# Four buffers for the late modulation weights, roots finished on VectorE, one weight split taken ahead

## What is computed

```python
c_act = silu(c)
for layer in range(2):
    mod = c_act @ w_ada[layer] + b_ada[layer]            # 1024 x 3072: shift, scale, gate
    h = rms(x, norm_g[layer]) * (1 + scale) + shift
    ...                                                  # layer 0: gated delta; layer 1: w_ada_kv (1024 x 2048) too
    x = x + gate * y

def gdn_mixer(h, w_in, conv_w, ...):
    proj = h @ w_in                                      # 1024 x 4112
    qkv = silu(causal_conv(proj[..., :3072], conv_w))
    z = proj[..., 3072:4096]
    q = l2norm(q per head of 128) * 128 ** -0.5
    k = l2norm(k per head of 128)
    # chunks of 64 tokens: a triangular inverse for each chunk and head, then a scan over the chunks
    return (rms(o) * silu(z)) @ w_out
```

## Time and profile before

| | us |
|---|---|
| median of 3 runs | 1294.51 (1293.77 to 1295.87) |
| the profiled execution, device time | 1292.0 |
| span of its trace | 1290.1 |
| TensorE busy in it | 1199.9 (93%) |
| opening, to the start of block 1 on TensorE | 70.2 |
| blocks 1 to 5, the z stage and its waits, to the start of the inverses (first L2173) | 70.2 to 254.6 |
| inverses with the late modulation, to the start of the scan (first L2263) | 254.6 to 378.8 |
| scan and all later layers | 378.8 to 1290.1 |

### The profile page before, as it was taken

One profiled execution on the slowest core, in us unless ns is written; L12 is line 12 of the kernel. 1 busy time (PEld: TensorE's weight loads), 2 busy tenths in 40 slices (PEclk: granted clock), 3 DMA queues, 4 the chain that ended last, 5 costly groups with the idle time before them and its releaser, 6 DMA issues.

```text
span 1290.1 us, 20510 instructions
## 1 busy us (share of the span) xinstructions
PE 1199.9 (93%) x8602; PEld 906.3 (70%) x8602; DVE 452.0 (35%) x852; ACT 541.0 (42%) x916; POOL 378.1 (29%) x150
## 2 busy tenths in 40 slices
PE   5899998989889889999998998989999999999989
PEld 3688875667658767777775656757887677777767
DVE  4575533343314214260214553140202333231563
ACT  4132238733326233452547663233134533654430
POOL 0134431322145442334431000423144213343331
PEclk7999998999999899999998999999999999999999
DMA  9533331156570221223321100233132412224201
GB/s 324 173 92 98 98 98 33 34 184 207 173 228 2 98 66 66 98 66 103 109 99 49 23 12 1 68 102 98 33 114 66 139 41 66 69 95 139 93 1 66
DMA packets 105613, 120.05 MB, mean 93 GB/s; under 512 B 5128, under 2 KB 91560, under 8 KB 105528
## 3 DMA queue, kind: packets, MB, share of 16 engines
q1 hardware_dynamic: 101280, 114.37, 28.0%
q10 hardware_dynamic: 4248, 4.45, 1.2%
HBM read 111.47 MB, written 2.10 MB: 88 GB/s over the span
## 4 chain that ended last, share of the span: by engine, by line
PE 82%; ACT 6%; DMA 4%; DVE 4%; issue 3%; SPq 1%; ACTq 0%; DVEq 0%
PE ps L1851 47%; PE ps L2545 4%; PE ps L2387 2%; PE ps L2396 2%; PE ps L1940 1%; DMA raw<-in_w_ada_kv_dram 1%; PE ps L2420 1%; PE ps L1974 1%; DMA raw<-in_w_ada_dram 1%; PE ps L2514 1%; PE ps L2027 1%; PE ps L2196 1%; PE ps L2501 1%; PE ps L2461 1%; PE ps L2607 1%
## 5 line engine op out<-in xcount | busy, mean ns | idle before, releaser
L556 POOL TENSOR_TENSOR wlo<-raw,whi 128x2048 fp32r<-128x2048 f32 x55 | 253.6, 4611 | 606.7 <-ACT whi L714 594.3
L714 ACT ACTIVATE whi<-raw 128x2048 fp32r<-128x2048 f32 x54 | 103.2, 1910 | 247.4 <-PE ps L1851 207.2
L562 POOL TENSOR_TENSOR wlo<-raw,whi 128x2048 fp32r<-128x2048 f32 x10 | 46.3, 4632 | 117.3 <-ACT whi L813 117.3
L1177 ACT ACTIVATE p<-sc,nmx 128x256 f32<-128x256 f32 x64 | 31.9, 501 | 57.9 <-DVE nmx L1682 57.9
L1851 PE MATMUL ps<-hC_hi,whi 128*128 128x512 f32 x208 | 52.9, 396 | 0.0
L1851 PE MATMUL ps<-hC_lo,whi 128*128 128x512 f32 x208 | 51.4, 389 | 0.0
L1851 PE MATMUL ps<-hC_hi,wlo 128*128 128x512 f32 x208 | 51.4, 389 | 0.0
L813 ACT ACTIVATE whi<-raw 128x2048 fp32r<-128x2048 f32 x12 | 23.0, 1916 | 63.8 <-PE ps L1851 63.8
L1851 PEld LDWEIGHTS ps<-hC_hi,whi 128*128 128x128 f32 x208 | 38.3, 188 | 14.9 <-issue 7.2
L1851 PEld LDWEIGHTS ps<-hC_lo,whi 128*128 128x128 f32 x208 | 39.0, 188 | 8.3
L1851 PEld LDWEIGHTS ps<-hC_hi,wlo 128*128 128x128 f32 x208 | 39.0, 188 | 8.1
(11 more groups left out here) (456 smaller groups left out, 2741.1 us busy)
## 6 DMA issues: line engine op xcount, KB each, us to landing
raw<-in_w_in_dram SPq DMA_DIRECT2D x24, 1024.0 KB, 5.1
raw<-in_w_in_a_dram SPq DMA_DIRECT2D x16, 1024.0 KB, 5.5
raw<-in_w_ada_dram SPq DMA_DIRECT2D x16, 1024.0 KB, 5.2
raw<-in_w_ada_kv_dram SPq DMA_DIRECT2D x8, 1024.0 KB, 5.7
raw<-in_w_kv_dram SPq DMA_DIRECT2D x8, 1024.0 KB, 5.3
raw<-in_w_in_b_dram SPq DMA_DIRECT2D x8, 1024.0 KB, 5.4
ada_a<-in_w_ada_dram SPq DMA_DIRECT2D x4, 1024.0 KB, 12.3
ada_b<-in_w_ada_dram SPq DMA_DIRECT2D x4, 1024.0 KB, 12.6
```

The costliest lines, as they stand in the source:

```text
L556: pool.tensor_tensor(wlo[:, s, :], raw[:, s, :], whi[:, s, :].bitcast(F32), ALU.subtract).then_inc(lo_ready, 1)
L562: pool.tensor_tensor(wlo[:, s, :], raw[:, s, :], whi[:, s, :].bitcast(F32), ALU.subtract).then_inc(lo_ready, 1)
L714: A(whi[:, s, :], raw[:, s, :], ACT.Copy).then_inc(hi_ready, 1)
L1177: A(p2[:, n % 2, 256 * e:256 * e + 256], sc2[:, n % 2, 256 * e:256 * e + 256], ACT.Exp, scale=-1.0, bias=nmx[:, grp, t, 2 * hp + e:2 * hp ...
```

## The change

Four edits, all in the first layer.

1. `late_w`, two further buffers of 1 MB in place of `hA_lo` (free once the z stage is multiplied). The late units of odd `ada` number go there, the others stay in `raw`. A load waits for the last use of its own buffer, which is now four units back; the first two of `late_w` wait for the end of block 7 (`dense_full`). They count on semaphores of their own (`ada_loaded[s]`). The loads of block 8 wait for units 20 and 21 in place of 22 and 23.
2. `root_halves` has one logarithm and two exponentials; `lengths` waits for both exponentials of the pair, copies the 64 rows of the root to the other half on VectorE, waits for its own copy (`roots_moved`), and multiplies.
3. The high part of block 1's first unit is taken between `hA_hi` tiles 5 and 6, behind a wait for its load. The GpSimd part has its place and its wait (`hi_ready`) unchanged.
4. GpSimd waits for `xin_done` 2 (both transposes of the first head pair) ahead of `decayed_queries(0)`.

```diff
+            with ExitStack() as s2:
+                sb("pad_lw", [128, KD * T], F32, s2)
+                late_w = sb("late_w", [128, 2, 2048], F32, s2)
...
+        def spare(what, n):
+
+            return what == "ada" and (n - EARLY) % 2 == 1
...
             def raw_free(r, s):
 
-                what, n = order[r - 1]
+                of = [load for load in order[:r] if spare(*load) == spare(*order[r])]
+                if not of:
+                    sp.wait_ge(dense_full, 4 * D_OUTA)
+                    return
+                what, n = of[-1]
                 sp.wait_ge(ada_done if what == "ada" else lo_ready, 2 * n + s + 1)
...
-                        dst = raw_ch(s)
-                    sp.dma_start(dst, src).then_inc(raw_loaded[s], 16)
+                        dst = late_src(n, s) if what == "ada" else raw_ch(s)
+                    sp.dma_start(dst, src).then_inc((ada_loaded if spare(what, n) else raw_loaded)[s], 16)
...
             restores(0, (0, 1))
+            pool.wait_ge(xin_done, 2)
             decayed_queries(0)
...
                 A(second, gdn_bank(g), ACT.Ln, bias=epsc).then_inc(ss_read, 2)
                 act.wait_ge(ss_read, g + 2)
-                A(first[64:128, :], second[0:64, :], ACT.Exp, scale=-0.5)
                 A(first[0:64, :], second[0:64, :], ACT.Exp, scale=-0.5).then_inc(r_ready, 1)
-                act.wait_ge(r_ready, g + 1)
-                A(second[0:64, :], second[64:128, :], ACT.Exp, scale=-0.5).then_inc(rh_read, 1)
-                act.wait_ge(rh_read, (g - G_GDN) // 2 + 1)
                 A(second[64:128, :], second[64:128, :], ACT.Exp, scale=-0.5).then_inc(r_ready, 1)
...
             for k in range(KD):
+                if k == KD - 2:
+                    act.wait_ge(raw_loaded[0], 32)
+                    A(whi[:, 0, :], raw[:, 0, :], ACT.Copy).then_inc(hi_ready, 1)
                 act.wait_ge(xr_done, k + 1)
                 act.wait_ge(mods_pair, 2 * (k // 2) + 2)
                 A(hA_hi[:, k, :], xr[:, k, :], ACT.Identity, scale=amul[:, 0, k:k + 1],
...
             def lengths(t0, t1):
                 for t in range(t0, t1):
-                    dve.wait_ge(r_ready, G_GDN + t + 1)
+                    dve.wait_ge(r_ready, G_GDN + t - t % 2 + 2)
+                    here, there = side(t % 2), side(1 - t % 2)
+                    copy(rbuf[there, (G_GDN + t) % 2, :], rbuf[here, (G_GDN + t) % 2, :]).then_inc(roots_moved, 1)
+                    dve.wait_ge(roots_moved, t + 1)
                     STT(qkvT[:, t, :], qkvT[:, t, :], 128.0 ** -0.5 if t < HG else 1.0, rbuf[:, (G_GDN + t) % 2, :],
                         ALU.mult, ALU.mult).then_inc(qkn_done, 1)
```

More of the change, by code:

```diff
@@ L293, in raw_ch, with raw_count, spare_count, late_src @@
             return raw[:, s, :].rearrange("p (k n) -> p k n", k=KD)
+        def spare(what, n):
+            return what == "ada" and (n - EARLY) % 2 == 1
+        def raw_count(what, n):
+            return 16 * sum(not spare(*load) for load in order[:load_of[what, n] + 1])
+        def spare_count(n):
+            return 16 * (1 + (n - EARLY + 1) // 2)
+        def late_src(n, s):
+            return late_w[:, s, :].rearrange("p (k n) -> p k n", k=KD) if spare("ada", n) else raw_ch(s)
         def modrow(o):
```

17 lines of the change are left out of this document (10 added, 7 removed).

## The result

The kernel before took 1295.19 us in the median beside the changed kernel (1293.77 to 1296.70, 4 runs), the changed kernel 1278.91 us (1275.07 to 1286.65, 4 runs). The ratio is 0.9882, with a 95% interval of 0.9834 to 0.9930. Its profiled execution took 1279.78 us, with a span of 1277.8.

A forecast was written before the change was run, and what follows sets the result against it. TensorE carries 82% of the chain, so only its standstills pay. Gains of 5.6 + 0.6 + 1.0 + 10.8 = 18.0 us take the median from 1294.5 to 1276.5 us, range 1272.0 to 1283.0.

The forecast's parts named there:

- The four waits that I chose: TensorE's waits: 4.92 us in the opening, 5.21 before block 7, 4.19 before the inverses, 10.8 for late modulation weights.
- Opening, -5.6: Block 1's first unit split ahead: tile 7's low part no longer held, no clock drop; block 1 starts 5.6 us earlier.
- Roots, -0.6: z stage: two exponentials fewer per pair against two VectorE copies of 0.42 us; z_silu(0) 0.6 us earlier.
- rival 3: z stage: GpSimd's split goes ahead of VectorE's fourth scaling and holds it, delaying the gates; 1279.5 us, chance 0.12.
- Queries, -1.0: Before the inverses: GpSimd's queries no longer hold a select, -1.0 us; bound +0.2 if select L1472 is held beside them.
- Four buffers, -10.8: Late units, 270 to 378 us: loads may start four units before, so all ten DMA waits go, 10.8 us.
- each wait is saved whole: Late units: at each of the ten waits the other engine was done before the weights, so nothing replaces the wait.
- rival 1: Late stretch: waits without releaser, from many short TensorE instructions, take back 5.8 us; 1282.3 us, chance 0.14.
- Rival 2: Late stretch: the 2.9 us wait without releaser goes too, 2.9 and 1.3 us more gained; 1272.3 us, chance 0.08.
- Rivals 4 and 5: 4: single queue makes the buffers useless, 1287.3 us, chance 0.05; 5: seven 2.9 us waits, slower, 1296.8 us, chance 0.01.
- Behind the scan, as long as before: Layers behind the scan: the scan starts 18.0 us earlier, and all behind it takes as long as before, 911 us.
- The signs of being wrong: Waits without releaser growing between 255 and 370 us, or a first unit's copy waiting for its load.

The follow-up runs named there:

- no_opening_split: The changed kernel with block 1's first weight copy put back behind tile 8, the other three edits kept; 1285.93 us, 0.9924 of the kernel before.
- after_third: The changed kernel run once more, unchanged, in the third group of experiments; 1277.28 us, 0.9846 of the kernel before.
- after_again: The changed kernel run once more, unchanged, in the first group of experiments; 1280.19 us, 0.9885 of the kernel before.
- four_exponentials: The changed kernel with the roots as before (four exponentials on ScalarE, no copies on VectorE); 1277.51 us, 0.9839 of the kernel before.
- z_wait: The changed kernel with GpSimd's second z block split waiting for six norm inputs; run twice, 1277.81 and 1273.39 us, 0.9854 and 0.9824 of the kernel before.
- no_pool_wait: The changed kernel without GpSimd's wait for the transposes' inputs ahead of the decayed queries; 1282.11 us, 0.9902 of the kernel before.
- two_buffers: The changed kernel with all late units in the two raw buffers again (no late_w); 1288.94 us, 0.9936 of the kernel before.

## Why the prediction was right, and where it was off

- **What bounds the kernel**: right. The four waits that I chose were the four that changed, and the scan starts 15.0 us earlier in the first profile.
- **Opening, -5.6**: right; 4.25 us of wait and 1.35 of clock by no_opening_split, less up to 0.7 for a hold that I put at 0.1; 5.5 at block 1 in the kernel after. Two details were off. The load was issued 0.6 us later than in the kernel before and landed as much later, so the copy waited for it (0.84 us, and 0.43 in after_third) and began at 47.45 and not at 47.2. And L1292, now L1313, was held 0.76 us and not 0.1, since the split ended at 54.05 and not at 53.7, and since VectorE came to it 0.6 us earlier than before (53.15, not 53.77). TensorE came 0.7 us later to tile 6 for it. In after_third the hold was 0.36 (0.52 less 0.16) and cost 0.3; in after_again, where the split ended at 53.56, it was nothing. In the first profile the TensorE clock hid this: the kernel before was at half clock from 18 to 35 us and this one wasn't.
- **Roots, -0.6**: mechanism right, size off; 0.2 to 0.3. The step that failed is the gate product, which I had ending 0.2 us earlier. The split did start 0.16 earlier measured from block 1, but took 4.80 us in place of 4.60, so the product ended where it had. It began at 198.40, while VectorE's last scaling of the pair (198.05 to 198.74) ran, which the two copies had put there; in four_exponentials, where VectorE was idle at its start, it took 4.62. So the likely reason is the same hold the other way round, which I had left out; no run tests it apart. I had the fourth logarithm 0.7 later, and it was 1.07. The chain through the held product was right; I priced the edit in it, but didn't say that removing the hold would be worth ten times as much as the edit (2.8 against 0.25). The hold of 2.94 us stood in the earlier trace rows, and z_wait shows what it was worth. The new copies did take 0.42 us, and rival 3 didn't occur in the kernel after: the split went ahead of no copy there, 4.03 us behind the second logarithm, with VectorE's fourth scaling at 3.68. (204.04 - 198.70 - 1.3 is 4.04 and not 4.02, which changes nothing.)
- **Queries, -1.0**: right, 1.05 us by no_pool_wait. The bound of +0.2 fell with the select beside the queries, which wasn't held.
- **Four buffers, -10.8**: the ten waits for DMA went, as forecast, and the step "each wait is saved whole" failed. The late stretch fell by 8.4 us in the kernel after (117.8 to 109.4), by 6.7 and 8.4 in the other two profiles. 2.6, 4.3 and 4.0 us came back as waits for instruction packets: 5.4 became 8.0, 9.7 and 9.4. That is rival 1 by its mechanism, at half to three quarters of its price of 5.8; so a rival that had a chance of 0.14 came true in part. Its two terms, what the waits come to and that TensorE takes many short instructions, were right; I wrote against it that one in 108 us is few, and left out that six smaller ones stood in the same list. Rival 2 fell too: the wait of 2.9 us did go where it was, but others came.
- **Rivals 4 and 5** fell: two_buffers' waits are not in the changed kernel, and no seven waits of 2.9 us came.
- **Behind the scan, as long as before**: right for the work (907.5 and 908.0 in two profiles, 907.7 before), and 2.8 us off in the profile that came with the result, by its clock.
- **The signs of being wrong**: both came. Waits without a releaser grew, and that is the step that failed. A first unit's copy waited for its load, at almost no cost.
- **The sum**: 18.0 forecast; the median fell by 16.3, 16.3 and 20.4 us in the three comparisons with the kernel before (the one of the result, after_again's and after_third's). At the scan's start the three profiles give 15.0, 14.3 and 14.5. Of the 3.0 missing in the first, 2.4 are from the buffers, 0.35 from the roots, and 0.1 each from the opening and from the stretch between block 7 and the inverses. So the change is worth 14.3 to 15.0 us where it acts. The medians' 16.3 and more, and with them the 2.4 us by which the forecast was missed and not 3 or more, owe something to the scatter of totals; the range would have been met either way.

## What to carry to other kernels

- When a queue of loads is the bound of a stretch, ask what else comes over the same DMA engines. Here a stretch of 2630 short matmuls took a packet of instructions every 5 us, and TensorE waited for some of them as soon as loads filled the same engines. Sum up all waits without a releaser and look for a packet that lands shortly before each ends. More instructions made the waits longer and less traffic ended them; whether fewer, longer instructions would shorten them was not tried.
- An engine that is sped up gains nothing ahead of an instruction that another engine holds. Find the hold first: here one wait for GpSimd gave 2.8 us at block 7, and made an edit that had been worth 0.25 us worth 1.3.
- Judge edits of 1 or 2 us by stages of the profile, from a start that both kernels share, since totals move by several us with clock and races.

The version with all four parts and the z stage's wait took 0.9824 and 0.9854 of the kernel before, the changed kernel 0.9846 to 0.9885. In the group that had both it was 3.9 us less; taken over all groups the intervals overlap, and what is shown is that its block 7 starts 2.8 us earlier.

## What the runs showed of the hardware that was not expected

- TensorE's waits without a releaser: 8.0 to 9.9 us in a stretch with the DMA engines busy at 0.70, 0.5 us with 0.02, 13.7 us with 192 matmuls more. The long ones end 1.1 to 1.6 us after a 16 KB packet of the instruction queue lands, in one program ahead of the same few matmuls, a number of times about 127 apart.
- VectorE's hold lasts over a row of GpSimd instructions, not one: 6.40 us for a subtraction that takes 0.68, behind a cast and four products. By the records a start 0.06 us earlier decided it, in one of the thirteen profiles. The Trainium skill's page "SBUF — State Buffer", in the section on the two separate sides, has the lock held for a whole instruction; this trace agrees, and here the waiting engine did not get in between five instructions in a row either.
- A copy of 64 rows by 512 in fp32, from one half of the partitions to the other, took VectorE 0.42 us, where 128 rows by 512 subtract in 0.68.
- Three profiles of one program, with the same 4632 matmuls behind the scan, had 38.4, 28.5 and 29.0 us there at 1.2 GHz, and took 910.5, 908.0 and 907.5 us.
